# The attention gates' tile of the input projection: high and low weights in one block, and its place ahead of the query tiles

## The chip, the cores and the metric

The kernel runs on one core of a Trainium2 chip. The metric is the device time of one execution in microseconds, lower is better. The profile gives times from the start of the span, which is the time from the first to the last instruction.

## The reference, cut to what matters

One step of a hybrid decoder layer: a prompt of 1024 rows and 8 sampled sequences of 4 rows are normalised and multiplied by one weight matrix of 1024 rows. Its columns hold the queries, three pairs of keys and values, 24 gate columns, and the two halves of a convolution input.

```python
def mixer_inputs(x, g, w_in):
    B, T = x.shape[:2]
    proj = rmsnorm(x, g) @ w_in
    cuts = [int(c) for c in np.cumsum([Q_COLS, KV_COLS, KV_COLS, KV_COLS, GATE_COLS])]
    q, kc, ks, kw, gt, cv = jnp.split(proj, cuts, axis=-1)
    kv = lambda a: a.reshape(B, T, 2, N_KV_HEADS, HEAD_DIM)
    gates = jax.nn.sigmoid(gt.astype(F32)).reshape(B, T, 3, N_HEADS)
    a, b = jnp.split(cv, 2, axis=-1)
    u = a * jax.nn.sigmoid(b)
    return q.reshape(B, T, N_HEADS, HEAD_DIM), kv(kc), kv(ks), kv(kw), gates, u
```

After it, cached keys and values go page by page through a small two-layer network ("compression"), then come attention, the output projection and an MLP.

## The kernel before, in words

**The projection.** All 1056 rows (1024 of the prompt, 32 sampled) are held transposed as `Ahi` and `Alo`, the rounded value and what the rounding left. The matrix is cut into 19 tiles of 128 columns, listed in `TILES` and numbered t = 0 to 18. A tile's weights come by DMA into the one buffer `win_raw`; ScalarE rounds them to `win_hi`, VectorE subtracts and writes `win_lo`. TensorE then makes three kinds of product, `win_hi`·`Ahi`, `win_hi`·`Alo` and `win_lo`·`Ahi`: 3 kinds x 8 blocks of 128 input rows x 3 stretches of 352 columns = 72 matmuls a tile (`group`, L862). Tile t goes to PSUM bank group t % 2. ScalarE's `epilogue` takes it out and raises `free[t % 2]`. Tiles 14 to 17 are the four query tiles and tile 18, the last, is the gate tile, of whose 128 columns 24 are kept. In the last tile the order of the products is `Alo`, `Ahi`, then `win_lo`, so that `Alo`'s memory comes free early.

**Side work in the tiles.** `IN_TILE` says which small jobs TensorE does between the matmuls of a tile. `rows0` to `rows8` turn keys and values back to rows (six transposes each, L904); three of them stand in each of tiles 14, 15 and 16. ScalarE copies them to `rowbuf`, and SP's DMA queue stores them (`store_rows`). The order in which ScalarE, VectorE and SP do their parts is that of the code for each engine, and each engine does its instructions in that order.

**SP's queue.** Its order is written by hand: weights of the tiles, stores of rows, `spill_q(g)` (the g-th query tile goes to HBM; it waits for `free` of that query tile), and the loads of the cached pages. A group of eight pages is a "quad" (`load_quad`). Quads go in halves of four DMAs of 128 KB; quad 0 is read back from the stored prompt rows and, like quad 1, comes through SP alone. Of quads 2 and on SP brings one half and GpSimd (POOL) the other. The order on SP is: `spill_q(2)`, quads 1 and 0, `store_rows(8)`, `spill_q(3)`, quads 2, 3 and 4, the sampled gates' DMAs, quads 5 and on.

**From a quad to the compression.** VectorE's `relay(g)` (L1250, four copies) brings quad g into order. TensorE's `turn` (L933) transposes it, ScalarE writes `Xhi` (L713), VectorE `Xlo` (L1234), and TensorE's `layer1` (L1008) multiplies them. `turn(0, ...)`, which needs `relay(0)`, stands inside the last projection tile, four groups before its end. `turn(2, 0)` needs quads 1 and 2, `turn(2, 1)` quads 3 and 4.

**The gates.** ScalarE applies the sigmoid to the gate tile's 24 rows and writes `gT`; TensorE transposes it (L1063, eight small transposes) after the first unit of the compression, and VectorE copies it to `gate_p`. The sampled rows of `gT` go through HBM to `gate_s`.

Of the kernel before, what the change touches and what calls it, by code (L numbers as in the profile page):

```python
# [207 lines left out]
def three(ap):  # L208
# [16 lines left out]
         ("kv", KS), ("kv", KW), ("q", 0), ("q", 1), ("q", 2), ("q", 3), ("gate", 0)]  # L225
# [5 lines left out]
AUX = ([f"xn{r}" for r in range(NR)] + [f"xT{r}" for r in X_KEPT_ORDER[1:]] + ["state", "conv"] + [f"rows{r}" for r in range(NR)] + ["gate"])  # L231
IN_TILE = {1: ("xT6", "xT7"), 2: ("xT8", "xT2"), 3: ("xT3", "xT4"), 4: ("xT5", "xT1"), 6: ("state",), 12: ("conv",),
           14: ("rows0", "rows1", "rows2"), 15: ("rows3", "rows4", "rows5"), 16: ("rows6", "rows7", "rows8")}
# [9 lines left out]
def aux(name):  # L243

    return AUX.index(name)

# [31 lines left out]
def front(c):  # L278
# [15 lines left out]
    gT = c.at("gT", [P, R], F32, RSTD_OFF)  # L294
# [19 lines left out]
    warm = c.at("warm", [P, 1], F32, REST_OFF + 1280)  # L314
# [62 lines left out]
    zeroed, qb_ready, gate_kept, g_moved = c.sem("sampled_zeroed"), c.sem("qb_ready"), c.sem("gate_kept"), c.sem("gates_moved")  # L377
# [14 lines left out]
    with (nc.psum_tensor("ps_a", [P, 512], F32) as ps_a, nc.psum_tensor("ps_b", [P, 512], F32) as ps_b,  # L392
# [41 lines left out]
        def _(sp):  # L434
# [46 lines left out]
            weights(16)  # L481
            for r in range(3):
                store_rows(r)
            spill_q(0)
            weights(17)
# [3 lines left out]
            weights(18)  # L489
# [133 lines left out]
        def _(act):  # L623
# [60 lines left out]
            def epilogue(t):  # L684
# [31 lines left out]
            def pe_high(cc):  # L716
# [3 lines left out]
                                     ACT.Copy).then_inc(pe_hi, 1)  # L720

# [30 lines left out]
            for t in range(2, NT):  # L752
                if t + 1 < NT:
                    W.split_hi(act, t + 1, (t + 1) % 2, 2)
                for name in IN_TILE.get(t, ()):
                    if name == "state":
                        keep_state()
                    elif name == "conv":
                        keep_conv()
                    elif name[:2] == "xT":  # L760
# [18 lines left out]
                if t == 18:  # L779
# [3 lines left out]
                    for e in range(KVH):  # L783
                        for g in range(G):
                            h = G * e + g
                            i = nc.scalar.activation(c.QB[DH * e:DH * e + DH, :, NEW * h:NEW * h + NEW],
                                                     c.proj[DH * e:DH * e + DH, g, T:R].rearrange("p (b t) -> p b t", t=NEW), ACT.Copy)
                    i.then_inc(qb_ready, 1)
# [8 lines left out]

            pe_high(1)
# [2618 lines left out]
```

## Time and profile before

| what | value |
|---|---|
| median of 3 runs | 1847.2 us (1843.07 to 1852.34) |
| profiled execution, its time | 1847.21 us |
| profiled execution, its span | 1845.6 us |
| TensorE busy | 1790.0 us, 97% of the span |
| VectorE, ScalarE, GpSimd busy | 1057.8, 721.9, 746.8 us |
| mean granted clock of TensorE | 0.994 of full speed |

"Busy" counts the time in which an engine has an instruction under way. Matmuls overlap in the records (one of 352 columns is shown with some 320 ns, and the next begins about 160 ns after it), so the pace of TensorE is read from the starts of its instructions.

### The profile page before, as it was taken

What the parts mean: (1) busy time and instruction counts of PE and PEld (TensorE: products, weight loads), DVE (VectorE), ACT (ScalarE), POOL (GpSimd) and SP (SyncE); (2) the same over time, 40 slices, a digit from 0 to 9 for tenths busy, and PEclk for the clock granted to TensorE, in tenths of its full rate; (3) what the DMA queues carried; (4) which work ended last, traced back from release to release, by engine and by line L of the source; (5) the groups of instructions that cost most, each with busy time, mean ns of one, the idle gap of its engine ahead of it and who ended that gap; (6) DMA issues with size and microseconds to landing.
All of it is one profiled execution on the core that took longest, in us unless ns stands there. A gap on an engine that the chain in (4) does not pass through costs nothing.

```text
span 1845.6 us, 36000 instructions
## 1 busy us (share of the span) xinstructions
PE 1790.0 (97%) x13796; PEld 1671.7 (91%) x13796; DVE 1057.8 (57%) x1802; ACT 721.9 (39%) x1355; POOL 746.8 (40%) x702
## 2 busy tenths in 40 slices
PE   8999999999998999999998999999999999999998
PEld 7999999999986667676998999999989999999998
DVE  6799965685557677767548754544532222224525
ACT  5312333345346576666425333333421112114435
POOL 2204972233304343444544756565422323225531
PEclk9999999999999999999999999999999999999999
DMA  4421375345413543342414223222542223112214
GB/s 155 129 69 47 112 203 152 101 127 149 98 62 119 147 124 121 119 135 71 140 46 146 105 105 116 98 100 105 183 145 69 97 68 115 41 53 91 58 35 140
DMA packets 178793, 198.31 MB, mean 107 GB/s; under 512 B 22580, under 2 KB 152304, under 8 KB 178103
## 3 DMA queue, kind: packets, MB, share of 16 engines
q1 hardware_dynamic: 168173, 172.67, 30.2%
q0 software_dynamic: 7840, 21.25, 4.1%
q10 hardware_dynamic: 2610, 2.10, 0.4%
q8 instruction: 110, 1.80, 0.4%
q14 instruction: 60, 0.49, 0.1%
HBM read 165.00 MB, written 35.55 MB: 109 GB/s over the span
## 4 chain that ended last, share of the span: by engine, by line
PE 58%; DVE 5%; issue 2%; POOL 2%; ACT 2%; DMA 1%; SPq 0%; ACTq 0%; DVEq 0%; POOLq 0%
PE ps L198 13%; PE ps L2643 11%; PE ps L204 6%; PE ps L2648 5%; PE ps L2416 5%; PE ps L3248 3%; PE ps L1825 3%; PE ps L1837 3%; PE ps L1813 2%; POOL S L1780 2%; PE ps L1864 2%; PE ps L3258 1%; DVE S L2074 1%; PE ps L3274 1%; PE ps L1900 1%
## 5 line engine op out<-in xcount | busy, mean ns | idle before, releaser
L3059 DVE TENSOR_TENSOR xT<-ps,xT 128x1056 f32<-128x1056 f32 x40 | 50.3, 1258 | 271.5 <-PE ps L204 271.5
L184 POOL TENSOR_TENSOR wd_lo<-wd_raw,wd_hi 128x1024 fp32r<-128x1024 f32 (+1 forms) x40 | 99.1, 2478 | 261.9 <-ACT wd_hi L2957 261.9
L1780 POOL TENSOR_SCALAR S<-S,inv,gate_p 128x640 f32<-128x640 f32 (+7 forms) x186 | 124.9, 689 | 191.6 <-DVE inv L2084 191.6
L198 PE MATMUL ps<-Hhi,wd_hi 128*128 128x352 f32 x768 | 168.0, 327 | 9.5 <-DVE Hlo L3023 5.0
L198 PE MATMUL ps<-Hlo,wd_hi 128*128 128x352 f32 x768 | 166.8, 325 | 0.0
L1164 DVE SCALAR_TENSOR_TENSOR y<-u,conv_w,y 128x1024 f32<-128x1024 f32 x120 | 156.5, 1351 | 1.2
L198 PEld LDWEIGHTS ps<-Hhi,wd_hi 128*128 128x128 f32 x768 | 132.2, 191 | 10.4 <-DVE Hlo L3023 5.6
L1008 PE MATMUL ps_p<-Xhi,w1hi 128*128 128x256 f32 x544 | 139.0, 293 | 1.4 <-ACT Xhi L713 1.4
L431 POOL DMA_DIRECT2D raw<-in_cache_cmp_kv_dram x124 | 77.9, 631 | 150.2 <-DVE relaid L1250 121.6
L2957 ACT ACTIVATE wd_hi<-wd_raw 128x1024 fp32r<-128x1024 f32 (+1 forms) x40 | 35.6, 890 | 249.2 <-PE ps L204 246.3
L1008 PE MATMUL ps_p<-Xlo,w1hi 128*128 128x256 f32 x544 | 132.6, 283 | 0.0
L198 PEld LDWEIGHTS ps<-Hlo,wd_hi 128*128 128x128 f32 x768 | 132.0, 190 | 0.0
L204 PE MATMUL ps<-Hhi,wd_lo 128*128 128x352 f32 x768 | 129.4, 322 | 0.0
L204 PEld LDWEIGHTS ps<-Hhi,wd_lo 128*128 128x128 f32 x768 | 124.4, 189 | 0.0
L1234 DVE TENSOR_TENSOR Xlo<-ps_p,Xhi 128x512 fp32r<-128x512 f32 x132 | 85.1, 686 | 59.5 <-ACT Xhi L713 59.4
L713 ACT ACTIVATE Xhi<-ps_p 128x512 fp32r<-128x512 f32 x132 | 72.5, 598 | 105.7 <-PE ps_p L933 98.3
L1961 ACT ACTIVATE S<-S,mn 128x64 f32<-128x64 f32 (+8 forms) x180 | 109.0, 611 | 2.1 <-DVE mn L2074 2.1
L2643 PE MATMUL ps<-s_hi,up_hi 128*128 128x264 f32 x512 | 104.5, 285 | 1.7 <-DVE s_lo L2764 0.9
L862 PE MATMUL ps_p<-Ahi,win_hi 128*128 128x352 f32 x456 | 104.1, 328 | 1.5 <-DVE Alo L1141 1.5
L1008 PEld LDWEIGHTS ps_p<-Xhi,w1hi 128*128 128x128 f32 x544 | 103.4, 190 | 2.1 <-ACT Xhi L713 1.7
L2643 PE MATMUL ps<-s_lo,up_hi 128*128 128x264 f32 x512 | 103.7, 284 | 0.0
L862 PE MATMUL ps_p<-Alo,win_hi 128*128 128x352 f32 x456 | 103.7, 326 | 0.0
(475 smaller groups left out, 4502.5 us busy)
## 6 DMA issues: line engine op xcount, KB each, us to landing
s_raw<-in_cache_slc_kv_dram SPq DMA_DIRECT2D x256, 128.0 KB, 2.1
raw<-in_cache_cmp_kv_dram SPq DMA_DIRECT2D x132, 128.0 KB, 4.3
hidden<-cs SPq DMA_DIRECT2D x32, 528.0 KB, 2.6
Hraw<-hidden SPq DMA_DIRECT2D x32, 528.0 KB, 4.8
up_raw<-in_w_up_dram SPq DMA_DIRECT2D x16, 1024.0 KB, 5.4
raw<-in_cache_cmp_kv_dram POOLq DMA_DIRECT2D x124, 128.0 KB, 4.4
win_raw<-in_w_in_dram SPq DMA_DIRECT2D x38, 256.0 KB, 3.3
wd_raw<-in_w_down_dram SPq DMA_DIRECT2D x16, 512.0 KB, 4.1
```

The costliest lines, as they stand in the source:

```text
L184: self.c.nc.gpsimd.tensor_tensor(self.lo[s][:, 0:nk, :], self.raw[s % self.raw_slots][:, 0:nk, :], self.hi[s][:, 0:nk, :].bitcast(F32), AL ...
L198: nc.tensor.matmul(ps[:, j, 0:CH], self.hi[s][:, k, :], x(k)[:, CH * j:CH * j + CH], start=(k == 0 and n == 0), stop=False)
L204: mm = nc.tensor.matmul(ps[:, j, 0:CH], self.lo[s][:, k, :], xhi(k)[:, CH * j:CH * j + CH], start=False, stop=(k == nk - 1))
L862: mm = nc.tensor.matmul(ps[t % 2][:, j, 0:CH], w[t % 2][:, k, :], x[:, k, CH * j:CH * j + CH], start=(m == 0), stop=(m == NG - 1))
L1008: mm = nc.tensor.matmul(ps_h[n % 2][:, 0:w], ws[cc][:, j, :], x[n % 2][:, j % 8, slice(j // 8, j // 8 + w)], start=(j == 0 and m == 0), st ...
L1164: i = V_.scalar_tensor_tensor(out=y, in0=x, scalar=w, in1=y, op0=ALU.mult, op1=ALU.add)
L1234: V_.tensor_tensor(Xlo[n % 2][x], ps_x[v % 2].rearrange("p (n j) -> p j n", j=8), Xhi[n % 2][x].bitcast(F32), ALU.subtract).then_inc(lo_re ...
L1780: nc.gpsimd.tensor_scalar(x, x, inv[:, n % 3, 3 * e + br:3 * e + br + 1], c.gate_p[:, i, H * br + h:H * br + h + 1], ALU.mult, ALU.mult).t ...
L1961: nc.scalar.activation(x, x, ACT.Exp, bias=mn[:, n % 3, e, br, part:part + 1], scale=-1.0, accum_out=sums[:, n % 3, 3 * e + br:3 * e + br ...
L2416: mm = nc.tensor.matmul(banks[t % 2][:, j, 0:CH], w[t % 2][:, k, :], x(k)[:, CH * j:CH * j + CH], start=(n == 0 and m == 0), stop=(n == KT ...
L2643: nc.tensor.matmul(ps[:, bank + j, 0:HC], w_hi[s % 4][:, k, :], ops[m][:, k, c0 + HC * j:c0 + HC * j + HC], start=(k == 0 and m == 0), sto ...
L2648: mm = nc.tensor.matmul(ps[:, bank + j, 0:HC], w_lo[s % 4][:, k, :], ops[0][:, k, c0 + HC * j:c0 + HC * j + HC], start=False, stop=(k == K ...
```

## The change

The list of tiles puts the gate tile at t = 14, and the queries at t = 15 to 18. For the gate tile VectorE writes the low weights of columns 0 to 31 into columns 32 to 63 of `win_hi` itself, and TensorE multiplies that block of 64 columns by `Ahi` and `Alo`: 2 x 8 x 3 = 48 matmuls. Result rows 0 to 23 and 32 to 55 hold the two parts. ScalarE copies the 64 rows to `gate_parts`, and nine small products with a constant matrix `gate_sum`, inside tile 15, add the halves and transpose them; ScalarE applies the sigmoid to what they give. The side jobs `rows0` to `rows8` move to tiles 15, 16 and 17, and SP's loads of weights stand earlier in its list. The part low x low is added to the sum as well.

```diff
-         ("kv", KS), ("kv", KW), ("q", 0), ("q", 1), ("q", 2), ("q", 3), ("gate", 0)]
+         ("kv", KS), ("kv", KW), ("gate", 0), ("q", 0), ("q", 1), ("q", 2), ("q", 3)]
...
-           14: ("rows0", "rows1", "rows2"), 15: ("rows3", "rows4", "rows5"), 16: ("rows6", "rows7", "rows8")}
+           15: ("gate", "rows0", "rows1", "rows2"), 16: ("rows3", "rows4", "rows5"), 17: ("rows6", "rows7", "rows8")}
+SIDE_AT = {1: (5,), 2: (5, 12), 3: (5, 12, 19), 4: (4, 9, 14, 19)}
...
             weights(16)
+            weights(17)
             for r in range(3):
                 store_rows(r)
             spill_q(0)
-            weights(17)
+            weights(18)
             for r in range(3, 6):
                 store_rows(r)
             spill_q(1)
-            weights(18)
             for r in range(6, 8):
                 store_rows(r)
             spill_q(2)
...
-            sp.wait_ge(free[0], 10)
+            both_read(sp, "gate")
             for e in range(3):
                 sp.dma_start(g_dram[e].rearrange("g (b h t) -> h (g b) t", h=H, t=NEW),
-                             gT[H * e:H * e + H, T:R].rearrange("h (b t) -> h b t", t=NEW)).then_inc(g_moved, 16)
+                             g_new[H * e:H * e + H, :].rearrange("h (b t) -> h b t", t=NEW)).then_inc(g_moved, 16)
...
-                elif kind == "gate":
-                    act.wait_ge(w1_lo, 2)
-                    nc.scalar.activation(three(gT[0:3 * H, :]), ps[t % 2][0:3 * H, :, 0:CH], ACT.Sigmoid).then_inc(free[t % 2], 1)
+                else:
+                    nc.scalar.activation(three(g_parts[:]), src[0:GATE_ROWS], ACT.Copy).then_inc(free[t % 2], 1)
+
+            def keep_gate():
+                act.wait_ge(turned[0], aux("gate") + 1)
+                nc.scalar.activation(c.gate_p[:].rearrange("p q g -> p (q g)"), ps_a[:, 0:24 * QB], ACT.Sigmoid).then_inc(read[0], 1)
+                act.wait_ge(turned[1], aux("gate") + 1)
+                nc.scalar.activation(g_new[:], ps_b[0:3 * H, 0:SR], ACT.Sigmoid).then_inc(read[1], 1)
...
+            act.wait_ge(free[0], 10)
+            keep_queries(G - 1).then_inc(qb_ready, 1)
             pe_high(1)
...
+                elif kind == "gate":
+                    pe.wait_ge(free[GATE_TILE % 2], GATE_TILE // 2 + 1)
+                    pe.wait_ge(masked, 12)
+                    begin(0, name)
+                    for m in range(QB):
+                        mm = nc.tensor.matmul(ps_a[:, 24 * m:24 * m + 24], g_parts[:, P * m:P * m + P], g_sum[:], start=True, stop=True)
+                    mm.then_inc(turned[0], 1)
+                    begin(1, name)
+                    nc.tensor.matmul(ps_b[0:3 * H, 0:SR], g_sum[:], g_parts[:, T:R], start=True, stop=True).then_inc(turned[1], 1)
...
+            def gate_tile(t):
+                pe.wait_ge(W.lo_ready, t + 1)
+                for k in range(KT):
+                    for n, x in enumerate((Ahi, Alo)):
+                        for j in range(NCH):
+                            mm = nc.tensor.matmul(ps[t % 2][0:GATE_ROWS, j, 0:CH], W.hi[t % 2][:, k, 0:GATE_ROWS], x[:, k, CH * j:CH * j + CH],
+                                                  start=(k == 0 and n == 0), stop=(k == KT - 1 and n == 1))
+                mm.then_inc(W.done, 1)
...
-                if n == 1:
-                    pe.wait_ge(free[0], 10)
-                    begin(0, "gate")
-                    for r in range(QB):
-                        mm = nc.tensor.transpose(ps_a[:, 24 * r:24 * r + 24], gT[0:24, P * r:P * r + P], c.ident[0:24, 0:24])
-                    mm.then_inc(turned[0], 1)
...
+                if t == GATE_TILE:
+                    V_.tensor_tensor(W.hi[t % 2][:, :, 32:64], W.raw[0][:, :, 0:32], W.hi[t % 2][:, :, 0:32].bitcast(F32), ALU.subtract).then_inc(W.lo_ready, 1)
+                    return
...
-                if n == 2:
-                    dve.wait_ge(turned[0], aux("gate") + 1)
-                    dve.wait_ge(g_moved, 48)
-                    V_.tensor_copy(c.gate_p[:].rearrange("p q g -> p (q g)"), ps_a[:, 0:24 * QB]).then_inc(gate_kept, 1)
```

TensorE's instructions from the side job of `rows8` to the first matmul of the compression stand so before. The last rows with `win_hi_161` and `win_lo_163` are the gate tile (t = 18); the `x24` row with `win_lo_164` ends tile 17.

```order
L904 MATMUL ps_a<-ident,proj 32x128 x4
L904 MATMUL ps_b<-ident,proj 32x128 x2
L862 MATMUL ps_p<-Ahi,win_lo_163 128x352 x12
...
L862 MATMUL ps_p<-Ahi,win_lo_164 128x352 x24
L862 MATMUL ps_p<-Alo,win_hi_161 128x352 x24
L862 MATMUL ps_p<-Ahi,win_hi_161 128x352 x24
L862 MATMUL ps_p<-Ahi,win_lo_163 128x352 x15
L933 MATMUL ps_p<-ident,relaid_129 128x128 x8
L862 MATMUL ps_p<-Ahi,win_lo_163 128x352 x9
L1008 MATMUL ps_p<-Xhi_133,w1hi_118 128x256
```

And so in the changed kernel, where tile 18 is the last query tile:

```order
L930 MATMUL ps_a<-ident,proj 32x128 x4
L930 MATMUL ps_b<-ident,proj 32x128 x2
L879 MATMUL ps_p<-Ahi,win_lo_166 128x352 x12
L879 MATMUL ps_p<-Alo,win_hi_163 128x352 x24
L879 MATMUL ps_p<-Ahi,win_hi_163 128x352 x24
L879 MATMUL ps_p<-Ahi,win_lo_165 128x352 x15
L968 MATMUL ps_p<-ident,relaid_131 128x128 x8
L879 MATMUL ps_p<-Ahi,win_lo_165 128x352 x9
```

Between `rows8` and the last tile there stood one whole tile (17) without side jobs; now the last tile follows at once.

SP's queue around the third and the fourth spill of queries stands so before (`bank0_free` and `bank1_free` are `free[0]` and `free[1]`; the third spill waits for tile 16, the fourth for tile 17):

```order
L479 DMA q_spill<-proj 128x1056 [waits bank0_free]
L426 TENSOR_LOAD pages [waits bank_b_written,pages_loaded]
...
L431 DMA raw_125<-out_prompt_cmp_dram 64x512 [waits rows_sent1,rows_sent0]
L431 DMA raw_125<-out_prompt_cmp_dram 64x512 x3
...
L479 DMA q_spill<-proj 128x1056 [waits bank1_free]
L426 TENSOR_LOAD pages [waits bank_b_written,sampled_u_ready,conv_step]
```

And so in the changed kernel:

```order
L484 DMA q_spill<-proj 128x1056 [waits bank1_free]
L431 TENSOR_LOAD pages [waits bank_b_written,pages_loaded]
...
L436 DMA raw_127<-out_prompt_cmp_dram 64x512 [waits rows_sent1,rows_sent0]
L436 DMA raw_127<-out_prompt_cmp_dram 64x512 x3
...
L484 DMA q_spill<-proj 128x1056 [waits bank0_free]
L431 TENSOR_LOAD pages [waits bank_b_written,sampled_u_ready,conv_step]
```

The order is the same; the two waits are now for tile 17 (bank 1) and tile 18 (bank 0), each one tile later.

## Rows read from the trace of the kernel before

**Rows 1.** The page: span and busy time.

```profile
span 1845.6 us, 36000 instructions
...
PE 1790.0 (97%) x13796; PEld 1671.7 (91%) x13796; DVE 1057.8 (57%) x1802; ACT 721.9 (39%) x1355; POOL 746.8 (40%) x702
```

**Rows 2.** Timeline of TensorE at tiles' ends: start, us, instructions, [idle before].

```profile
193.88 4.04 PE L862 MATMUL ps_p<-Ahi,win_lo 128*128 128x352 f32 x24
197.76 0.65 PE L862 MATMUL ps_p<-Ahi,win_hi 128*128 128x352 f32 x3
...
238.39 0.63 PE L862 MATMUL ps_p<-Ahi,win_hi 128*128 128x352 f32 x3
...
249.96 4.04 PE L862 MATMUL ps_p<-Alo,win_hi 128*128 128x352 f32 x24
...
260.14 1.03 PE L933 MATMUL ps_p<-ident,relaid 128*128 128x128 f32 x8
260.93 1.71 PE L862 MATMUL ps_p<-Ahi,win_lo 128*128 128x352 f32 x9
264.04 0.35 PE L1008 MATMUL ps_p<-Xhi,w1hi 128*128 128x256 f32 x1 [1.40 <-ACT Xhi L713]
```

**Rows 3.** Timeline of TensorE: small transposes and products behind the projection.

```profile
270.78 0.67 PE L1063 MATMUL ps_a<-ident,gT 24*128 24x24 f32 x8
271.38 1.09 PE L933 MATMUL ps_p<-ident,relaid 128*128 128x128 f32 x8
...
284.19 0.34 PE L1026 MATMUL ps_p<-hid,w 128*64 128x64 f32 x4
284.45 1.09 PE L933 MATMUL ps_p<-ident,relaid 128*128 128x128 f32 x8
```

**Rows 4.** Timeline of VectorE: weights of tile 14, relays of quads 0, 4 and 5.

```profile
191.65 1.48 DVE L1181 TENSOR_TENSOR win_lo<-win_raw,win_hi 128x1024 fp32r<-128x1024 f32 x1
...
257.03 1.47 DVE L1250 COPY relaid<-raw 128x512 f32<-128x512 f32 x4 [5.94 <-DMA raw<-out_prompt_cmp_dram]
...
276.56 1.47 DVE L1250 COPY relaid<-raw 128x512 f32<-128x512 f32 x4 [3.38 <-DMA raw<-in_cache_cmp_kv_dram]
...
303.64 2.77 DVE L1250 COPY relaid<-raw 128x512 f32<-128x512 f32 x8
```

**Rows 5.** Timeline of SP's queue: when each group of DMAs is issued.

```profile
239.76 0.33 SPq L479 DMA_DIRECT2D q_spill<-proj  x1
242.13 6.69 SPq L431 DMA_DIRECT2D raw<-in_cache_cmp_kv_dram  x8
...
257.89 0.35 SPq L479 DMA_DIRECT2D q_spill<-proj  x1
260.12 11.79 SPq L431 DMA_DIRECT2D raw<-in_cache_cmp_kv_dram  x12
...
275.42 6.45 SPq L431 DMA_DIRECT2D raw<-in_cache_cmp_kv_dram  x8
```

**Rows 6.** Waits of SP's queue, 190 to 330 us: total, times, longest.

```profile
SPq L479 <- ACT proj L693: 5.7, 3, 4.7
```

**Rows 7.** Timeline of ScalarE: what it does behind tiles 16 and 18.

```profile
238.59 1.15 ACT L693 ACTIVATE proj<-ps_p,qscale 128x1056 f32<-128x1056 f32 x1 [0.87 <-PE ps_p L862]
...
263.82 1.02 ACT L696 ACTIVATE gT<-ps_p 24x1056 f32<-24x1056 f32 x1
```

**Rows 8.** Timeline of TensorE at its longest gap of the stage.

```profile
278.77 1.85 PE L933 MATMUL ps_p<-ident,relaid 128*128 128x128 f32 x8 [3.42 <-DVE Xlo L1234]
280.27 0.56 PE L1008 MATMUL ps_p<-Xhi,w1hi 128*128 128x256 f32 x1
```

**Rows 9.** Stretches: us, engines' busy time (instructions), granted clock, DMA share, GB/s.

```profile
258.00:262.00 4.00, 4.00 (x30) 3.98 (x29) 2.98 (x7) 0.00 (x0) 1.31 (x3) 1.00 1.07 330
280.00:282.00 2.00, 2.00 (x11) 2.00 (x11) 1.40 (x3) 1.01 (x2) 1.82 (x4) 0.50 0.94 253
```

**Rows 10.** DMA issues, 235 to 300 us: count, KB each, median us to landing.

```profile
raw<-in_cache_cmp_kv_dram SPq DMA_DIRECT2D x36, 128.0 KB, 3.1
```

More of the change, by code:

```diff
@@ L230 @@
 X_KEPT_ORDER = (0, 6, 7, 8, 2, 3, 4, 5, 1)
-AUX = ([f"xn{r}" for r in range(NR)] + [f"xT{r}" for r in X_KEPT_ORDER[1:]] + ["state", "conv"] + [f"rows{r}" for r in range(NR)] + ["gate"])
+AUX = ([f"xn{r}" for r in range(NR)] + [f"xT{r}" for r in X_KEPT_ORDER[1:]] + ["state", "conv", "gate"] + [f"rows{r}" for r in range(NR)])
+GATE_TILE = TILES.index(("gate", 0))
+GATE_ROWS = 64
 IN_TILE = {1: ("xT6", "xT7"), 2: ("xT8", "xT2"), 3: ("xT3", "xT4"), 4: ("xT5", "xT1"), 6: ("state",), 12: ("conv",),
-           14: ("rows0", "rows1", "rows2"), 15: ("rows3", "rows4", "rows5"), 16: ("rows6", "rows7", "rows8")}
+           15: ("gate", "rows0", "rows1", "rows2"), 16: ("rows3", "rows4", "rows5"), 17: ("rows6", "rows7", "rows8")}
+SIDE_AT = {1: (5,), 2: (5, 12), 3: (5, 12, 19), 4: (4, 9, 14, 19)}
 NQD = NPG // 8
@@ L293, in front @@
     crow = c.at("crow", [SR, 2, C], F32, RSTD_OFF)
-    gT = c.at("gT", [P, R], F32, RSTD_OFF)
+    g_parts = c.at("gate_parts", [GATE_ROWS, R], F32, PROJ_OFF + 4224 * 3)
+    g_new = c.at("gate_new", [3 * H, SR], F32, REST_OFF + 1152)
+    g_sum = c.at("gate_sum", [GATE_ROWS, 3 * H], F32, REST_OFF + 1280)
     rs = c.at("ln_rs", [P, R], F32, RSTD_OFF)
@@ L313, in front @@
     x_rstd = c.at("x_rstd", [P, NR], F32, REST_OFF + 1216)
-    warm = c.at("warm", [P, 1], F32, REST_OFF + 1280)
+    warm = c.at("warm", [P, 1], F32, REST_OFF + 1376)
     g_row = c.at("g_row", [1, D], F32, W1_OFF + 7296 + 4096)
@@ L376, in front @@
     rows_sent = [c.sem(f"rows_sent{s}") for s in range(2)]
-    zeroed, qb_ready, gate_kept, g_moved = c.sem("sampled_zeroed"), c.sem("qb_ready"), c.sem("gate_kept"), c.sem("gates_moved")
+    zeroed, qb_ready, g_moved = c.sem("sampled_zeroed"), c.sem("qb_ready"), c.sem("gates_moved")
     alo_read, q_out, c.q_back = c.sem("a_lo_read"), c.sem("q_spilled"), c.sem("q_back")
@@ L720, in pe_high, with keep_queries @@
                                      ACT.Copy).then_inc(pe_hi, 1)
+            def keep_queries(g):
+                for e in range(KVH):
+                    h = G * e + g
+                    i = nc.scalar.activation(c.QB[DH * e:DH * e + DH, :, NEW * h:NEW * h + NEW],
+                                             c.proj[DH * e:DH * e + DH, g, T:R].rearrange("p (b t) -> p b t", t=NEW), ACT.Copy)
+                return i
             act.wait_ge(made, 5)
@@ L759, in _ @@
                         keep_conv()
+                    elif name == "gate":
+                        keep_gate()
                     elif name[:2] == "xT":
@@ L782, in _ @@
                     act.wait_ge(free[0], 9)
[L783 to L788, printed above, removed]
+                    for g in range(G - 1):
+                        keep_queries(g)
                     act.wait_ge(alo_read, 1)
@@ L965, in _ @@
                 pe.wait_ge(free[t % 2], t // 2)
-                sides = dict(zip((5, 12, 19), IN_TILE.get(t, ())))
+                if t == GATE_TILE:
+                    gate_tile(t)
+                    continue
+                names = IN_TILE.get(t, ())
+                sides = dict(zip(SIDE_AT[len(names)], names)) if names else {}
                 for m in range(NG):
@@ L1040, in norm @@
                     if j == 0:
-                        pe.wait_ge(gate_kept, 1)
+                        pe.wait_ge(read[0], aux("rows8") + 1)
                     nc.tensor.matmul(ps_a[:, 0:CH], c.ones[:], lsq[:, 0, :], start=True, stop=True).then_inc(ln_summed, 1)
@@ L1116, in constants @@
                 V_.tensor_copy(peT[:], ps1[:, 2, 192:224]).then_inc(masked, 1)
+                V_.tensor_reduce(g_sum[:], c.ident[0:GATE_ROWS, 0:GATE_ROWS].rearrange("p (q i) -> p i q", q=2)[:, 0:3 * H, :], AX_X, ALU.add).then_inc(masked, 1)
             def variance(r):
@@ L1180, in weights_low @@
                 dve.wait_ge(W.hi_ready, t + 1)
+                if t == GATE_TILE:
+                    V_.tensor_tensor(W.hi[t % 2][:, :, 32:64], W.raw[0][:, :, 0:32], W.hi[t % 2][:, :, 0:32].bitcast(F32), ALU.subtract).then_inc(W.lo_ready, 1)
+                    return
                 V_.tensor_tensor(W.lo[t % 2][:], W.raw[0][:], W.hi[t % 2][:].bitcast(F32), ALU.subtract).then_inc(W.lo_ready, 1)
```

## The prediction

> **What bounds the kernel now.** I read the page first: TensorE is busy for 1790.0 of 1845.6 us [rows 1], so an edit that takes matmuls away should pay unless it makes TensorE wait. Then I read TensorE's timeline through the projection, because that is the stage changed. Its tiles follow each other without a gap: 24 matmuls take from 193.88 to 197.76, 3.88 us or 0.162 us each, and the last tile runs from 249.96 to the end of its last nine matmuls at 262.64 [rows 2]. Two gaps come behind it: 1.40 us before the compression's first matmul [rows 2], and 3.42 us before 278.77 [rows 8]. Last I read the timelines of VectorE and SP, to see how close the pages' transfers are to being late. They are very close. Relay 0 starts at 257.03, after a wait of 5.94 us for quad 0, and ends at 258.50 [rows 4]; TensorE uses it at 260.14 [rows 2]. That is 1.6 us of slack. Relay 4 starts at 276.56 after a wait of 3.38 us for its DMA [rows 4], and the gap before 278.77 is that wait, seen from TensorE. So at the end of this stage the bound is not TensorE but SP's queue, and the question is what the change does to that queue.
>
> **The change, part by part.**
>
> *Matmuls removed.* The gate tile goes from 72 to 48 matmuls of 352 columns. The 24 that go are worth 3.88 us, the time of 24 in the row [rows 2]. Half as many result rows don't shorten a matmul, as all 352 columns still stream. The tile needs its low weights at its first matmul instead of at its 49th. Before, tile 14's were begun at 191.65 and took 1.48 us, and the tile starts at 197.76 [rows 2, 4]: that wait is covered with 4.6 us to spare.
>
> *Products added.* Nine small float32 products, inside tile 15, on TensorE's path. No row has their shape. Below lie the gate transposes of before, eight in 0.60 us (270.78 to 271.38), 0.075 each; nine make 0.7 us. Above lie the 128x128 transposes at the longer reading of 1.09 us for eight, taken twice because the float32 products of L1026 are recorded as two matmuls each: 9 x 0.22 = 2.0 us [rows 3]. The nearest row is L1026 itself, two products in 0.26 us (284.19 to 284.45). I take 9 x 0.13 = 1.2 us.
>
> *Work moved.* The gate transposes at 270.78 go (0.60 us), and VectorE's copy of the gates. Both stand just ahead of the gap that the late quad 4 makes [rows 3, 8], so they give nothing. VectorE's subtraction for the gate tile shrinks to a quarter, about 1 us of an engine that then waits for DMA anyway [rows 4]. The nine row jobs move with tiles 15 to 17, together. ScalarE's two sigmoids lie in its waits between tiles. All this is costed at nothing.
>
> *SP's queue, first wait.* This is the term that decides. SP's third query spill waits for ScalarE to empty that query's tile, and all page loads are queued behind it. Before, tile 16 ends at 238.39 [rows 2], the spill goes out at 239.76, quad 1 from 242.13 with quad 0 behind it [rows 5], and relay 0 begins at 257.03 [rows 4]: 18.6 us behind the tile's end, and ready 20.1 us behind it. One of SP's three waits at the spills was 4.7 us long [rows 6], so SP does stand still there and isn't merely late. Now that spill waits for tile 17. Tile 17 ended at 249.96; it will end 3.88 - 1.2 = 2.7 us sooner, at 247.3. Relay 0 is then ready at 247.3 + 20.1 = 267.4. TensorE reaches its use, 10.2 us into the last tile, at 260.14 - 2.7 = 257.4. It waits 10.0 us, with the rest of the tile behind it. That rest takes 2.50 us (260.14 to 262.64), so the projection ends at 269.9 at full clock, against 262.64.
>
> *The clock behind that wait.* After the gap of 3.42 us the granted clock is 0.50 in 280 to 282 [rows 9], the level of 1.2 GHz, and the eight transposes take 1.50 us (278.77 to 280.27) instead of some 0.95 [rows 3, 8]. A gap of 10 us should do the same. All of the 2.50 us at half speed would cost at most another 2.5; the transposes cost 0.6 more, and nine matmuls bound by 352 columns about 1.2 more, if only their stream of columns doubles. I take 1.5 us: the projection ends at 271.4, which is 8.8 later than before. The Trainium skill ("TensorE: Matmul & The Clock Gate", "HAM oscillation — how this bites in real kernels") says that a wait for DMA drops the engine to half rate and that each burst after it starts cold. By that rule alone the term would be the whole 1.8 us, 0.3 more than I take; the trace agrees with the rule in its 0.50.
>
> *SP's queue, second wait.* The fourth spill now waits for the last tile. ScalarE emptied tile 18 from 1.18 us behind its end (263.82 against 262.64) [rows 2, 7]; with the 1.15 us that a query's epilogue takes there and 2.23 us from a spill to the next page load (257.89 to 260.12) [rows 5], quads 2 to 4 begin 4.7 us behind the end, at 276.1. Before they began at 260.12, while tile 18 still ran. From their first DMA to relay 4 it was 16.4 us (260.12 to 276.56) [rows 4, 5]. That is the upper bound. The lower is 12 DMAs at quad 1's pace, 12 x 6.69 / 8 = 10.0, and the median landing of 3.1 us [rows 5, 10]: 13.1. Before, the DMA engines were full for part of it (1.07) [rows 9]; now POOL's halves of quads 2 and 3 have long landed. I take 15.0. Relay 4 starts at 291.1, 14.5 us later than at 276.56. The Trainium skill ("DMA: Bandwidth & Descriptors", "Issuing engines are not separate DMA queues") says that the queues share the same 16 engines, so that loads from POOL would slow SP's. By that rule alone, with POOL's halves of quads 4 and 5 still falling in, the 16.4 would stay and the sum be 1.4 more.
>
> *Further on.* Quad 5's relay is at 303.64 [rows 4], and SP's half is issued from 275.42, in 6.45 us for quads 5 and 6 [rows 5]: some 18 us of slack, kept when both shift. TensorE is busy for 97% of the span [rows 1], so there is little idle time that could give the delay back.
>
> **The sum.** The 3.88 saved and the 1.2 added are both inside the 14.5, since the chain was counted from tile 17's end. The profiled execution took 1847.21 us, 1.6 more than its span and the same as the median of 1847.2: 1847.2 + 14.5 = 1861.7.
>
> **Rivals.**
>
> *A, forecast, 0.70.* Both waits, 1861.7. With warm clock, 0.7 for the products and 13.1: 14.5 - 1.5 - 0.5 - 1.9 = 10.6. With 0.3 more for the clock, 2.0 for the products and 16.4: 14.5 + 0.3 + 0.8 + 1.4 = 17.0. So 1857.8 to 1864.2.
>
> *B, only the first wait counts, 0.15.* SP catches up and quads 2 to 4 land as early behind the last tile as before. Then the delay is the 8.8 us of the first wait: 1856.0. For it: DMA is less crowded. Against it: SP starts them 4.7 us behind the tile's end, where it started 2.5 before it, 7.2 us lost. It holds only if the 15.0 falls below 9.3, less than issuing alone took.
>
> *C, not slower, 0.07.* The first transfers are in time: quad 0 does not depend on the spill as I read it, or is covered. Then 3.88 - 1.2 are saved, and the transposes' 0.6 at most: 1844.2. It decides from one point: relay 0 would have to be ready at 257.4, 10.0 us sooner. For it is only that the stores of rows 0 to 7, the true source of quad 0, are done well before; against it is SP's order.
>
> *D, more waits, 0.08.* The late start goes on to quads 5 to 8, or the half clock falls on more of the compression: another 5 us, 1867. Against: 18 us of slack.
>
> **How the numbers follow.** 0.5% (9.2 us) is about what a measurement of this kernel can tell from no change. Slower by more: all of A, D, and some of B, 0.81. Within: most of B, most of C, 0.16. Faster: 0.03. Range for 8 in 10: 1855.0 to 1867.0, which holds A with its bounds, the upper half of B and D's price.
>
> **What would show it.** In the profile after: 48 matmuls with 64 columns at 0.162 us each; nine products of 0.7 to 2.0 us; the third spill on SP near 248.6 and page loads from 251; TensorE idle some 10 us ahead of the first transposes of `relaid`, put down to the relay; the clock 0.50 behind it; the fourth spill near 273.8; relay 4 near 291, and all that follows 14.5 later. What would make it wrong: a first gap well under 10 us (quad 0 lands faster than 20.1 us behind tile 17), or relay 4 that waits for no DMA.

## The result and the profile after

The changed kernel takes 1864.9 us (median of 5 runs, 1862.46 to 1865.4), the kernel before, timed beside it, 1845.4 us (5 runs, 1843.07 to 1852.34). The ratio is 1.0093, with a 95% interval of 1.0074 to 1.0112: slower by 13.7 to 20.7 us. The profiled execution took 1864.73 us, 17.5 more than that of before (1847.21).

The page of the changed kernel, span and busy time:

```profile
span 1863.1 us, 35973 instructions
PE 1792.1 (96%) x13782; PEld 1672.0 (90%) x13782; DVE 1056.4 (57%) x1802; ACT 721.5 (39%) x1357; POOL 746.7 (40%) x702
```

The span is 17.5 us longer than in [rows 1], and TensorE is busy for 2.1 us more although it has fewer matmuls. So most of the loss is idle time, and some matmuls take longer. To find where, I looked for a mark that both programs pass, TensorE's first matmul of `ln_sq` behind the first part of the compression. First before, then after:

```profile
304.43 0.75 PE L1042 MATMUL ps_a<-ln_sq,ones 128*128 128x352 f32 x2
```

```profile
322.22 0.75 PE L1081 MATMUL ps_a<-ln_sq,ones 128*128 128x352 f32 x2
```

The mark is 17.8 us later, and from it to the end of the span there are 1541.2 us before and 1540.9 after. The delay arises ahead of the mark, and nothing later gives any of it back. 0.7 us of it stand already at tile 14 (198.42 against 197.76), ahead of everything that was changed, so 17.1 us arise between tile 14 and the mark. The timeline of TensorE through the changed stretch, as in [rows 2, 3, 8]:

```profile
198.42 0.63 PE L938 MATMUL ps_p<-Ahi,win_hi 128*64 128x352 f32 x3
...
206.05 0.64 PE L879 MATMUL ps_p<-Ahi,win_hi 128*128 128x352 f32 x3
...
208.54 1.96 PE L919 MATMUL ps_a<-gate_sum,gate_parts 64*128 64x24 f32 x16
210.43 0.24 PE L922 MATMUL ps_b<-gate_parts,gate_sum 64*24 64x32 f32 x2
210.60 1.03 PE L879 MATMUL ps_p<-Alo,win_hi 128*128 128x352 f32 x3
211.42 1.08 PE L879 MATMUL ps_p<-Ahi,win_hi 128*128 128x352 f32 x3
...
250.46 3.96 PE L879 MATMUL ps_p<-Alo,win_hi 128*128 128x352 f32 x24
...
271.83 1.97 PE L968 MATMUL ps_p<-ident,relaid 128*128 128x128 f32 x8 [11.24 <-DVE relaid L1287]
273.45 2.73 PE L879 MATMUL ps_p<-Ahi,win_lo 128*128 128x352 f32 x9
277.58 0.36 PE L1047 MATMUL ps_p<-Xhi,w1hi 128*128 128x256 f32 x1 [1.40 <-ACT Xhi L723]
...
289.22 1.00 PE L968 MATMUL ps_p<-ident,relaid 128*128 128x128 f32 x4 [4.37 <-DVE relaid L1287]
...
296.81 1.94 PE L968 MATMUL ps_p<-ident,relaid 128*128 128x128 f32 x8 [2.54 <-DVE Xlo L1271]
```

Read from the top: the gate tile's 48 matmuls take 7.63 us (198.42 to 206.05), the nine products 2.06 us (208.54 to 210.60), and the three matmuls behind them 0.82 us (210.60 to 211.42), where three elsewhere take 0.48. The last tile begins at 250.46. Inside it TensorE stands for 11.24 us until quad 0 is relaid, and further on, in the compression, for another 4.37 and 2.54. Three stretches (busy time of the engines with instructions, then granted clock, DMA share, GB/s): behind the products, across the first wait, and behind it:

```profile
210.60:214.10 3.50, 3.50 (x15) 3.50 (x14) 3.50 (x4) 0.34 (x3) 3.27 (x4) 0.54 0.00 0
258.00:270.00 12.00, 2.60 (x17) 2.31 (x15) 0.00 (x0) 0.00 (x0) 1.10 (x3) 0.81 1.06 241
271.80:276.20 4.40, 4.35 (x17) 4.05 (x17) 2.46 (x5) 0.00 (x0) 0.00 (x0) 0.55 0.00 0
```

SP's queue, for [rows 5]:

```profile
251.83 0.33 SPq L484 DMA_DIRECT2D q_spill<-proj  x1
254.21 6.57 SPq L436 DMA_DIRECT2D raw<-in_cache_cmp_kv_dram  x8
260.88 5.03 SPq L436 DMA_DIRECT2D raw<-out_prompt_cmp_dram  x8
...
278.53 0.36 SPq L484 DMA_DIRECT2D q_spill<-proj  x1
280.81 10.91 SPq L436 DMA_DIRECT2D raw<-in_cache_cmp_kv_dram  x12
```

VectorE's relays, for [rows 4]:

```profile
270.34 1.43 DVE L1287 COPY relaid<-raw 128x512 f32<-128x512 f32 x4 [19.40 <-DMA raw<-out_prompt_cmp_dram]
...
294.63 1.43 DVE L1287 COPY relaid<-raw 128x512 f32<-128x512 f32 x4 [2.78 <-DMA raw<-in_cache_cmp_kv_dram]
```

Quad 1 is issued from 254.21 instead of 242.13, relay 0 starts at 270.34 instead of 257.03, and relay 4 at 294.63 instead of 276.56. Both hand-written waits of SP moved back one tile, and each is seen as a late quad.

### The profile page after: what moved, and what is told of

Its sections match the earlier page's. It is cut to its first block, busy times and chain, and to the rows that moved or that the text cites. A ratio compares the mean times of both kernels' runs of the same rounds, so it can differ in the third digit from the quotient of the medians.

```text
span 1863.1 us, 35973 instructions
## 1 busy us (share of the span) xinstructions
PE 1792.1 (96%) x13782; PEld 1672.0 (90%) x13782; DVE 1056.4 (57%) x1802; ACT 721.5 (39%) x1357; POOL 746.7 (40%) x702
## 4 chain that ended last, share of the span: by engine, by line
PE 58%; DVE 5%; ACT 2%; issue 2%; POOL 2%; DMA 1%; SPq 0%; ACTq 0%; DVEq 0%; POOLq 0%
PE ps L198 13%; PE ps L2676 11%; PE ps L204 6%; PE ps L2681 5%; PE ps L2449 5%; PE ps L1858 3%; PE ps L3281 3%; PE ps L1870 3%; PE ps L1846 3%; PE ps L1897 2%; POOL S L1813 1%; PE ps L3291 1%; DVE S L2107 1%; PE ps L3307 1%; ACT S L1994 1%
## 5 line engine op out<-in xcount | busy, mean ns | idle before, releaser
L3092 DVE TENSOR_TENSOR xT<-ps,xT 128x1056 f32<-128x1056 f32 x40 | 50.3, 1257 | 271.8 <-PE ps L204 271.8
L1047 PEld LDWEIGHTS ps_p<-Xlo,w1hi 128*128 128x128 f32 x544 | 103.9, 192 | 0.0
L879 PE MATMUL ps_p<-Ahi,win_hi 128*128 128x352 f32 x432 | 99.8, 330 | 1.5 <-DVE Alo L1175 1.5
```

The costliest lines, as they stand in the source:

```text
L879: mm = nc.tensor.matmul(ps[t % 2][:, j, 0:CH], w[t % 2][:, k, :], x[:, k, CH * j:CH * j + CH], start=(m == 0), stop=(m == NG - 1))
L1047: mm = nc.tensor.matmul(ps_h[n % 2][:, 0:w], ws[cc][:, j, :], x[n % 2][:, j % 8, slice(j // 8, j // 8 + w)], start=(j == 0 and m == 0), st ...
```

## The experiments

**The theories.** T, the forecast's: the loss comes from the place of the tile, through the two spills that stand ahead of the page loads on SP; the halves themselves cost and gain next to nothing. R1: the products and their surroundings on TensorE are the loss. R2: the spills are only the first thing in the way, and behind them another wait or the transfers themselves would be as late. Each median is compared with runs of the kernel before on the same chip; the mark is the `ln_sq` matmul above. A mark comes from one profile and is a rougher measure than the medians: over the 14 profiles tile 14 begins between 196.49 and 198.78 us, and from the mark to the span's end it is 1539.5 to 1545.9 us.

**Undo one wait, then the other, then both.** In the changed kernel the third spill goes behind the loads of quads 1 and 0 (first run), the fourth behind quad 3 (second), or both (third):

```diff
-            spill_q(2)
             for g in (1, 0):
...
             store_rows(8)
-            spill_q(3)
+            spill_q(2)
             for g in (2, 3, 4):
                 load_quad(sp, mybir.EngineType.SP, 0, g)
+                if g == 3:
+                    spill_q(3)
```

> The changed kernel, with the third query spill moved behind quads 1 and 0 and the stores of rows 8 on SP. My theory: SP's wait at that spill holds the page loads back. Quads 1 and 0 are then held only by the side job of rows 8 (TensorE ends it at 248.7) and the reading of page numbers, so they start near 250.4 instead of 254.21; relay 0 starts near 266.5 instead of 270.34, TensorE's wait of 11.24 us shrinks to about 7.4, and all behind it, relay 4 too, comes 3.8 us sooner: 1861. Rival (the wait is set by how long the transfers take, not by when they start): relay 0 stays near 270 and the time near 1865.

Third spill alone: 1860.3 us, ratio 1.008 (1.006 to 1.01). From its waits of SP's queue, its SP and its VectorE timeline:

```profile
SPq L420 <- PE ps_b L930: 1.6, 1, 1.6
```

```profile
250.80 6.57 SPq L436 DMA_DIRECT2D raw<-in_cache_cmp_kv_dram  x8
257.47 5.01 SPq L436 DMA_DIRECT2D raw<-out_prompt_cmp_dram  x8
```

```profile
268.03 1.43 DVE L1287 COPY relaid<-raw 128x512 f32<-128x512 f32 x4 [16.91 <-DMA raw<-out_prompt_cmp_dram]
```

The page loads begin 3.4 us sooner and relay 0 only 2.3, as quad 0's loads now take 6.4 us to land (more on this below). The first row says why the loads don't begin sooner still: L420 is `load_quad`'s own wait for quad 1, for the transposes of the side job `rows8`. That job is in tile 17 now, where it was in tile 16. So two things were a tile late, the spill and `rows8`, and the forecast knew of one.

> The changed kernel, with only the fourth query spill moved, behind quads 2 and 3 on SP. My theory of two waits in a row: the first stays at 11.2 us; quads 2 and 3 then start near 272 instead of 280.81, the spill goes out near 279.5, quad 4 behind it, and relay 4 starts near 288.5 instead of 294.63: 6 us less, 1859. Rival B of the prediction (only the first wait counts): no change, 1865.

Fourth spill alone: 1857.3 us, ratio 1.0052 (1.0035 to 1.0069). The first wait stays at 11.54 us, and the second goes; in VectorE's timeline relay 4 begins 8.5 us earlier than in the changed kernel:

```profile
281.37 1.43 DVE L1288 COPY relaid<-raw 128x512 f32<-128x512 f32 x4 [0.77 <-DMA q_spill<-proj]
283.85 1.43 DVE L1288 COPY relaid<-raw 128x512 f32<-128x512 f32 x4
286.15 1.51 DVE L1288 COPY relaid<-raw 128x512 f32<-128x512 f32 x4 [0.88 <-DMA raw<-in_cache_cmp_kv_dram]
```

> The changed kernel with both spills moved as in the two runs before. My theory: relay 0 near 266.5, relay 4 near 284 to 286, so 9 to 10.5 us less than the changed kernel: 1855. It doesn't come back to the kernel before, since rows 8 and their tile still come one tile nearer to the end. Rival (the two waits are one and the same): no better than the better of the two alone.

Both: 1855.7 us, ratio 1.0043 (1.0026 to 1.0059). The mark falls from 322.22 to 311.36, of which 2.4 us stand already at tile 17's end (248.08), the half clock behind the products among them, which this profile doesn't have. Quad 1 is issued from 248.22, 6.0 us sooner, but relay 0 is at 266.49, only 3.9 sooner, and TensorE still waits 9.76 us for it. By the medians about half of the loss is gone, by T; the other half isn't, by R2.

**The same moves in the kernel before**, as a control, so that a gain of the moves in themselves isn't taken for an undone loss:

> The kernel before with its own tiles and gates, and only the two query spills moved behind the page loads on SP. It tells whether SP's order was already the bound ahead of the change. My theory: yes. Quad 1 starts near 238.4 instead of 242.13, relay 4 near 273 instead of 276.56, and TensorE's gap of 3.42 us ahead of it and the half clock behind it go: about 4 to 5 us less, 1842. Rival (the transfers take as long, whenever they begin): relay 4 stays near 276 and the time near 1847.

1844.5 us (12 runs), ratio 0.9989 (0.9977 to 1.0001). Quad 1 is issued from 237.82, 4.3 us sooner than before, and relay 0 starts at 253.40 and waits no more for a DMA, but for TensorE, which still reads `Alo`. The mark moves by 2.0 us, of which 0.7 stand already at tile 14 (197.05). So of the 10.9 us by which the mark fell in the changed kernel, 2.4 are no work of the moves, some 1.3 they give in the kernel before too, and some 7 are undone loss. The control had been expected at 1842, and the gain of 4 to 5 us didn't come. The first move alone:

> The kernel before with the same order of SP's queue as in the run of halves beside it: the control for what the halves alone bring. My theory: TensorE gets to the first quads 3.9 us later than with the halves and makes up 1.5 us at the small products; the time is 1 to 2.5 us above the run of halves: 1844. Rival (the transfers set the end in both): the same time as the run of halves.

1846.5 us, ratio 0.999 (0.998 to 1.0001). Relay 4 waits 2.67 us for its DMA at 276.05, and the mark is at 303.83, with tile 14 at 197.95, 0.2 us later than before.

**The halves alone.** The gate tile is put back to t = 18, with its 48 matmuls; the nine products stand after the first unit of the compression, and SP's order is that of before:

```diff
-         ("kv", KS), ("kv", KW), ("gate", 0), ("q", 0), ("q", 1), ("q", 2), ("q", 3)]
+         ("kv", KS), ("kv", KW), ("q", 0), ("q", 1), ("q", 2), ("q", 3), ("gate", 0)]
-           15: ("gate", "rows0", "rows1", "rows2"), 16: ("rows3", "rows4", "rows5"), 17: ("rows6", "rows7", "rows8")}
+           14: ("rows0", "rows1", "rows2"), 15: ("rows3", "rows4", "rows5"), 16: ("rows6", "rows7", "rows8")}
...
-                for k in range(KT):
-                    for n, x in enumerate((Ahi, Alo)):
+                for n, x in enumerate((Alo, Ahi)):
+                    for k in range(KT):
...
+                        if (n, k) == (1, KT - 4):
+                            turn(0, 0)
+                            turn(0, 1)
...
+                if n == 1:
+                    side("gate")
```

> The halves alone: the gate tile of 48 matmuls with its nine small products, but last in the order, as in the kernel before, with SP's order and the side jobs as they were. My theory: the change of place made the kernel slower, and the 3.9 us of matmuls saved are lost in two waits, as quad 0 is ready at 258.5 and quad 4 at 276.5 whatever TensorE does: TensorE waits 2.2 us for relay 0 and 3 to 6 us for relay 4, and the time is that of the kernel before, 1847 (1845 to 1849). Rival one (the block of halves itself costs, by its products and by the clock): 1850 or more. Rival two (matmuls saved are time saved): 1843.5.

1846.5 us, ratio 0.9998 (0.9987 to 1.0009): no change. TensorE saves its 24 matmuls, comes to the transposes sooner, and waits for what it won. Its timeline shows both waits:

```profile
258.16 1.09 PE L975 MATMUL ps_p<-ident,relaid 128*128 128x128 f32 x8 [2.33 <-DVE relaid L1296]
...
277.33 1.68 PE L975 MATMUL ps_p<-ident,relaid 128*128 128x128 f32 x8 [2.50 <-DVE Xlo L1280]
```

This is the cleanest reading of the study: the same arithmetic costs nothing in the old place, so the 0.93% is due to the place and what moves with it (the nine products in tile 15, the row jobs, the waits in SP's queue).

> The halves with the tile last, and the third and fourth spills in a row behind quads 1 and 0, so that no spill lands late for relay 2 (it waited 4.04 us for one where the fourth spill stood behind quad 3). My theory: relay 2 starts near 266.5, TensorE's gaps of 1.42 and 1.01 us go, 2 us less than that run: 1842.5. Rival (the sum of transfers in this stage is the bound, so one wait takes the place of another): 1844.5.

> The kernel of halves with its tile last, and the two spills moved behind the page loads as well. My theory: with the quads some 3.7 us sooner, TensorE waits neither for relay 0 nor long for relay 4, and both savings show: relay 4 near 273, TensorE there at about the same time, 5 to 6 us less than the kernel before: 1841.5. Rival (transfers are the bound): no better than the kernel before with its spills moved.

With the third spill moved as well: 1846.8 us, ratio 0.9993 (0.9977 to 1.0008). With both: 1844.8, ratio 0.999 (0.998 to 1.0). 1842.5 and 1841.5 had been expected. The intervals leave room for some 4 us of gain and for none. The first of the two shows new waits in VectorE's timeline, and a stretch of 20 us the load of the DMA engines beside them:

```profile
265.11 1.43 DVE L1296 COPY relaid<-raw 128x512 f32<-128x512 f32 x4 [0.96 <-DMA raw<-in_cache_cmp_kv_dram]
269.60 1.46 DVE L1296 COPY relaid<-raw 128x512 f32<-128x512 f32 x4 [1.92 <-DMA raw<-in_cache_cmp_kv_dram]
273.52 1.47 DVE L1296 COPY relaid<-raw 128x512 f32<-128x512 f32 x4 [2.46 <-DMA raw<-in_cache_cmp_kv_dram]
```

```profile
256.00:276.00 20.00, 14.42 (x118) 13.56 (x117) 10.36 (x24) 7.58 (x15) 13.72 (x23) 1.00 1.04 287
```

Relays 2, 3 and 4 each wait for a transfer now, with the DMA engines recorded as full (1.04). In the run with both spills moved it is the spill that is late instead: relay 2 waits 4.04 us for `q_spill`, since it overwrites the memory of the queries. But waits in one profile are not the whole account, as this run's mark shows:

```profile
300.71 0.75 PE L1089 MATMUL ps_a<-ln_sq,ones 128*128 128x352 f32 x2
```

With tile 14 at 198.78 that is 101.9 us from tile 14 to the mark, where the kernel before has 106.7: 4.7 us less, near the 5 to 6 that had been expected of this run. The DMA share in its 256 to 276 us is 0.90, and 1.4 of the 4.7 us are lost again behind the mark. The median shows 2 us, with an interval from nothing to some 3.7. So whether this version gains a little is open, and that the transfers forbid it is not shown.

**The place kept, the loss undone.** The gate tile stays at t = 14. `rows0` and `rows1` go into that tile and the other row jobs one tile forward, the page loads stand ahead of three spills (first run). In the second, the fourth spill stands behind quad 3, and relay 2 waits only for the first two spills, relay 3 for the rest:

```diff
-           15: ("gate", "rows0", "rows1", "rows2"), 16: ("rows3", "rows4", "rows5"), 17: ("rows6", "rows7", "rows8")}
+           14: ("rows0", "rows1"), 15: ("gate", "rows2", "rows3", "rows4"), 16: ("rows5", "rows6", "rows7", "rows8")}
...
+            spill_q(1)
+            spill_q(2)
             for g in (2, 3, 4):
                 load_quad(sp, mybir.EngineType.SP, 0, g)
+                if g == 3:
+                    spill_q(3)
...
-                    dve.wait_ge(q_out, 16 * PAIRS)
-                    dve.wait_ge(qb_ready, 1)
+                    dve.wait_ge(q_out, 32)
+                    dve.wait_ge(qb_early, 1)
+                elif g == 3:
+                    dve.wait_ge(q_out_late, 32)
+                    dve.wait_ge(qb_ready, 1)
```

> The changed kernel with its tile at 14, with the row jobs begun inside the gate tile (two there, three in tile 15, four in 16), so that rows 8 are turned in tile 16 as before the change, and with the spills of queries 1 to 3 behind the page loads. My theory: the page loads start near 235 and are ready ahead of the last tile's use; TensorE's waits of 11.2, 4.4 and 2.5 us go. The matmuls saved (3.9) less the products (2.1) and the gap of before (3.4) are gained: 1841 to 1843. Rival (the tile's place as such is bad, since the last tile's epilogue is that of a query, and relay 2 waits for its spill): TensorE still waits some 5 us ahead of relay 2 and 4, 1848.

1849.7 us, ratio 1.0017 (1.0009 to 1.0026): still a small loss, 1.7 to 4.8 us by the interval, and not the gain I had expected (1841 to 1843). The first wait is gone, relay 0 starts at 251.73. The second has a new cause:

```profile
275.29 1.43 DVE L1289 COPY relaid<-raw 128x512 f32<-128x512 f32 x4 [8.29 <-DMA q_spill<-proj]
```

> As the run with the row jobs begun in the gate tile, with the fourth spill behind quad 3 in place of quad 4, and with relay 2 waiting only for the spills of queries 0 and 1, whose memory it takes (relay 3 waits for queries 2 and 3). In that run TensorE's only long gap was 7.84 us, put down to relay 2, which waited for the spill. My theory: that wait was the last of the cost of the place; without it relay 2 starts near 267, relay 4 near 272, no gap longer than 1.5 us stands between the last tile and 280, and the time is 1840 to 1842. Rival (the spill's transfer now makes relay 3 and 4 late instead): a gap of 3 to 5 us ahead of the second pair of quads, 1845.

1846.3 us, ratio 0.9991 (0.998 to 1.0001). Relay 2 is at 267.58 without a wait, and relay 4 now waits:

```profile
276.13 1.43 DVE L1296 COPY relaid<-raw 128x512 f32<-128x512 f32 x4 [4.44 <-DMA raw<-in_cache_cmp_kv_dram]
```

The mark is at 304.24, where it was at 304.43 before, with tile 14 at the same time in both (197.74 and 197.76). So in the changed place too the loss can be undone whole, or all but the 1.3 us that such moves gave in the kernel before, by moving what had come to wait for later tiles. The 1840 to 1842 that had been expected were not reached. In 256 to 276 us of this run the DMA share is 1.06.

**R1, from both sides.** Seven of the nine products left out, and on the other side 24 matmuls put back into the gate tile. Neither version computes the reference's gates; they only price the work:

```diff
-                    for m in range(QB):
+                    for m in (QB - 1,):
```

> The changed kernel with seven of its nine small products left out (the gates of seven blocks of rows are then not those of the reference). It prices them: 7 x 0.23 = 1.6 us if their cost is only their own time, and up to 1.7 us more if the half clock that stood behind them in the profile of the changed kernel goes with them: 1861.6 to 1863.3 against 1864.9. Rival (they are hidden by the waits behind): 1865.

1858.7 us (6 runs), ratio 1.0062 (1.0045 to 1.0079). That is some 6 us less than the changed kernel, where the products left out measure 1.5, and 3 us below the lower end of what was expected. The timeline of TensorE at the products:

```profile
207.83 0.40 PE L919 MATMUL ps_a<-gate_sum,gate_parts 64*128 64x24 f32 x2
208.16 0.24 PE L922 MATMUL ps_b<-gate_parts,gate_sum 64*24 64x32 f32 x2
208.32 0.75 PE L879 MATMUL ps_p<-Alo,win_hi 128*128 128x352 f32 x3
```

The mark is 5.7 us sooner. At tile 17's end it is 3.4 (247.05 against 250.46): 1.5 are the products left out, 1.7 the half clock behind them, which this profile doesn't have, and 0.7 stand already at tile 14 (197.71), less small stalls. The rest comes behind: relay 4 begins 23.6 instead of 24.3 us behind relay 0, and the mark 26.4 instead of 27.6 behind relay 4. The time to tile 14 and the clock differ from one execution to the next (below), so in the profile the step is partly theirs. That doesn't explain the medians, and the products' own share isn't settled.

```diff
-                    for n, x in enumerate((Ahi, Alo)):
+                    for n, x in enumerate((Ahi, Alo, Ahi)):
...
-                                                  start=(k == 0 and n == 0), stop=(k == KT - 1 and n == 1))
+                                                  start=(k == 0 and n == 0), stop=(k == KT - 1 and n == 2))
```

> The changed kernel with a third pass of 24 matmuls in the gate tile, 72 as before the change (they multiply the high rows of the input a second time, so the gates are not those of the reference). My theory: all that follows is chained to the end of tile 17, so the 24 matmuls cost their 3.8 us in full: 1868.7, relay 0 at 274.2. Rival (in this stage the transfers set the end by themselves, at their own hours): TensorE's wait shrinks by 3.8 us and the time stays near 1865.

1865.6 us, ratio 1.0093 (1.0075 to 1.0111), as near to the changed kernel as it could be, and 3.1 us below the 1868.7 that T gave. The profile has the products at 212.64, 4.1 us later, the full clock behind them, and the mark at 325.30, 3.1 later. With the 1.7 us of half clock that it lacks, that is 4.8, for 24 matmuls that take 3.9 there and a tile 14 that begins 0.2 later. So the profile says that their time is on the path, while the medians, 0.7 us apart, don't show it; their spread (1861.7 to 1868.6) is wide enough to hold it, and the profile is of the slowest of the four runs. R1 holds for a few microseconds and not for the 17.8.

## Why the prediction was right

The forecast was 1861.7 us, range 1855.0 to 1867.0, slower with 0.81; the kernel took 1864.9. Rival A, both waits, is what happened, but larger than A allowed: its own upper bound was 1864.2. The loss was forecast at 14.5 us and measured as 19.5 between the medians (17.5 between the profiled executions). The number looks nearer than that because the kernel before came out at 1845.4 in the runs beside it, 1.8 below the 1847.2 that the forecast started from. So the mechanism was right and the size somewhat short; the steps:

**Matmuls removed: right.** 48 take 7.63 us, 0.159 each, where 0.162 was taken from [rows 2]. Half the columns of weights gave no shorter matmul.

**Products added: the term was mis-sized.** 1.2 us were taken and 2.06 measured, just past the upper bound of 2.0. That bound was mis-worked: 1.09 us for eight transposes, taken twice, is 0.27 a product and 2.5 for nine, which would have held the 2.06; the 0.22 fits only the distance of their starts (271.38 to 272.23). The choice of the row of L1026 as the nearest failed: its products too are recorded as two matmuls each, but its weights are 64 columns wide (128*64) and those of the products 128 (64*128). The changed kernel has two weight loads for every product. The rows of the weight loads:

```profile
208.54 1.86 PEld L919 LDWEIGHTS ps_a<-gate_sum,gate_parts 64*128 64x128 f32 x16 [0.22 <-issue]
```

The eight products last as long as their 16 loads, 1.86 us of the 1.89 from 208.54 to 210.43, or 0.116 a load. So the loads go with the pace, and not the 24 columns streamed. The width of 128 columns alone isn't the reason, as the gate transposes of before had weights as wide (24*128) and took 0.075 each; no run separates width from rows and data. Behind them came 1.7 us of half clock that the forecast didn't have.

**Tile 17's end: 247.3 forecast, 250.46 measured.** 0.7 stand already at tile 14 (198.42 instead of 197.76), 0.9 are the products' size, 1.7 the clock behind them.

**First wait: right, by one of two causes.** From tile 17's end to relay 0 ready 20.1 us were carried over, and 21.3 measured (250.46 to 271.77); TensorE waited 11.24 us instead of 10.0. SP's part was exact, 1.37 us to the spill and 2.4 from there to the loads. The 1.2 us more are in the transfer: quad 0's loads take 5.5 us to land in the changed kernel, by the DMA issues of 240 to 320 us, and took 2.7 before, by those of 235 to 285:

```profile
raw<-out_prompt_cmp_dram SPq DMA_DIRECT2D x8, 128.0 KB, 5.5
```

```profile
raw<-out_prompt_cmp_dram SPq DMA_DIRECT2D x8, 128.0 KB, 2.7
```

POOL's halves of quads 2 and 3 don't stand in SP's queue. They were issued at 253.41 and 257.09 before, when quad 0's loads, begun at 248.93, were mostly out, and at 253.27 and 256.94 after, right among quads 1 and 0 (DMA share 1.06 in 258 to 270).

The Trainium skill ("DMA: Bandwidth & Descriptors", "Issuing engines are not separate DMA queues") says that all queues draw on the same 16 engines. I had used it for the second wait; it was the first where it bit, and the trace agrees with its 5.5 against 2.7. The other profiles bear it out. POOL's halves are issued between 251 and 261 us in all of them. Where quad 0's loads begin by 248.93 they land in 2.6 to 2.8 us (8 profiles); where they begin behind, it is longer, by and large the longer the nearer they stand to POOL's halves: 7.2 us from 254.89 (both spills moved), 6.4 and 5.4 from 257.47 (third spill moved, seven products out), 5.9 from 257.97 (fourth spill moved), 5.5 from 260.88, 4.7 from 263.54 (72 matmuls). A load of 512 KB by ScalarE (`w1raw`, at 254.46) stands among them too, and no run takes the two apart.

The forecast also named only the spill as the lock. The run with the third spill moved showed the second lock, `rows8`, 3.4 us in front of it. Rival C spoke of the rows' stores as done well before; the last row job isn't.

**The clock: right.** 0.55 in 271.8 to 276.2, where the level of 1.2 GHz is 0.50. The stretch of 2.50 us took 4.35: 1.85 more, where 1.5 was taken and 1.8 was the bound. Its split was off both ways: the eight transposes took 0.8 more, not 0.6, and the nine matmuls 1.0, not 1.2.

**Second wait: right, a little smaller.** From the first DMA to relay 4 it was 13.8 us (280.81 to 294.63), inside 13.1 to 16.4, where 15.0 was taken. POOL's halves had landed, as the step said: the DMA share in 270 to 281 is 0.13. Quads 2 to 4 begin 4.6 us behind the projection's end, which is also what the forecast's own rows add up to (1.18, 1.15 and 2.23); it wrote 4.7.

**The sum.** Relay 4 shifts by 18.07 us: the 14.5 forecast, 3.2 for tile 17's end, 1.2 for quad 0's transfer, 0.35 for the clock, less 1.2 for the second wait, which makes 18.05. The mark shifts by 17.8. Rival B would have left relay 4 unmoved behind the projection's end; the run with only the fourth spill moved is B made true (1857.3, forecast 1856.0), and it shows that the changed kernel isn't that case. Rival C's 1844.2 should have been 1843.9 by its own terms (3.88 less 1.2, and 0.6). D's further waits didn't come: from relay 4 to the mark it is 27.6 us, and was 27.9.

What stays open: by how much the products on their own slow the kernel, since the half clock behind them comes and goes; why the run with seven products left out gained some 6 us, and whether more is to be won in this stage with fewer bytes in flight, which no run tried.

## What to carry to other kernels

A tile's place in an order sets more than the order of the matmuls. Before a tile is moved, list every wait, on every queue, that is counted in tiles (the spill, and `rows8` behind it), and what stands behind each; here 3.9 us of TensorE's time were bought with waits of 11.2, 4.4 and 2.5 us, where one of 3.4 had stood. A queue that is moved back may not keep its own pace: what another engine issues on its own time can come to share the DMA engines with it (5.5 us to land instead of 2.7 here). And where several waits stand close together, removing one tends to uncover the next: six versions with spills moved, matmuls saved, or both, had medians within 0.15% of the kernel before. Five of them (and the run with the row jobs moved) had been expected 3 to 7 us below it. The DMA share in 256 to 276 us was 1.04 to 1.06 in four of the six, but 0.89 and 0.90 in the other two, so full DMA engines are a likely cause for some of them and not shown for all.

## What the hardware showed that I had not expected

**Half clock behind small products, in some executions.** Behind the nine products the granted clock fell to 0.54 (210.6 to 214.1) in the changed kernel and to 0.57 with the third spill moved, though TensorE was recorded busy throughout. With the fourth spill moved, with both, with 72 matmuls, and in the two runs with the row jobs moved, the same products in tile 15 were followed by 1.00: half clock in 2 of 7 profiles. The edits of the spills lie further on in the program, so it isn't tied to them. In the run with 72 matmuls:

```profile
214.70:218.20 3.50, 3.50 (x25) 3.48 (x24) 3.50 (x4) 0.68 (x3) 3.34 (x3) 1.00 0.00 0
```

25 matmuls run there in 3.50 us, and 15 in the changed kernel. The Trainium skill ("TensorE: Matmul & The Clock Gate", "HAM oscillation — how this bites in real kernels") tells of half rate after waits; here it came with no wait in front. What sets it no run here shows.

**A small float32 product is as dear as its two weight loads**: 0.23 us with 64 rows and 24 columns, against 0.075 for a transpose from 24 rows, which is recorded once [rows 3].

**Equal code reaches the same place up to 2.3 us apart.** TensorE's first matmul is at 2.4 us in the kernel before, at 3.5 in the changed one, and at either in versions of both. By tile 14 the difference is another: the three versions with the halves last, which have the same code up to there, begin it at 196.49, 197.20 and 198.78, and the run with both spills moved has the late start (3.52) and an early tile 14 (197.57). So two marks of two profiles are compared with their tile 14 beside them, and a difference of a microsecond or two between them means little.
